# Prompt attention scores of a hybrid decoder layer: products of high and low fp32r parts, with the rope part stacked to 128 rows, in place of plain fp32 products

## The reference

```
def mla_scores(q_lat, q_rope, ckv, krope):
    s = einsum('bthc,bsc->bhts', q_lat, ckv) + einsum('bthr,bsr->bhts', q_rope, krope)
    return s * SM_SCALE
# prompt: 8 heads, 512 queries in 4 blocks of 128, causal mask, softmax, then p @ ckv
# q_lat and ckv have 128 channels, q_rope and krope have 64
```

## Time and profile before

| | |
|---|---|
| time, median of 3 runs | 1330.19 us (1328.15 to 1334.08) |
| profiled execution, span | 1334.3 us |
| PE busy | 1303.3 us, 98% |
| PE weight loads busy | 1234.6 us, 93% |
| DVE busy | 959.7 us, 72% |
| ACT busy | 602.2 us, 45% |
| POOL busy | 145.2 us, 11% |
| attention heads in the trace | 482.67 to about 722 us |

### The profile page before, as it was taken

One profiled execution on the slowest core, in us unless ns is written; L12 is line 12 of the kernel. 1 busy time (PEld: TensorE's weight loads), 2 busy tenths in 40 slices (PEclk: granted clock), 3 DMA queues, 4 the chain that ended last, 5 costly groups with the idle time before them and its releaser, 6 DMA issues.

```text
span 1334.3 us, 30517 instructions
## 1 busy us (share of the span) xinstructions
PE 1303.3 (98%) x11657; PEld 1234.6 (93%) x11657; DVE 959.7 (72%) x1847; ACT 602.2 (45%) x1144; POOL 145.2 (11%) x275
## 2 busy tenths in 40 slices
PE   9999999999999999899999999999999999999997
PEld 8999999999999978788888888889899999999996
DVE  5999899985487655555555665575889998988556
ACT  5455555653365344444345233234654555565323
POOL 0000000000003105455552000000000000000000
PEclk9999999999999999899999999999999999999999
DMA  4232223332256637777777313414253222333322
GB/s 165 94 121 102 96 95 123 110 97 90 65 194 219 218 94 207 228 211 237 214 228 250 140 64 129 153 48 168 75 193 96 96 96 96 100 107 116 101 87 101
DMA packets 86234, 180.85 MB, mean 136 GB/s; under 512 B 12681, under 2 KB 47498, under 8 KB 84042
## 3 DMA queue, kind: packets, MB, share of 16 engines
q1 hardware_dynamic: 77898, 162.12, 36.5%
q0 software_dynamic: 8192, 16.79, 4.4%
HBM read 162.29 MB, written 16.57 MB: 134 GB/s over the span
## 4 chain that ended last, share of the span: by engine, by line
PE 79%; DVE 9%; SPq 3%; DMA 3%; issue 3%; ACT 3%; DVEq 0%; ACTq 0%
PE acc L1096 20%; PE acc L1181 15%; PE acc L1018 11%; PE acc L855 6%; PE bank_a L1096 6%; PE acc L1042 4%; PE acc L927 2%; SPq L482 2%; DVE w_lo L2331 1%; PE bank_a L1251 1%; PE acc L1299 1%; PE bank_a L1281 1%; DMA w_raw<-in_w_gu 1%; SPq L475 1%; PE acc L1321 1%
## 5 line engine op out<-in xcount | busy, mean ns | idle before, releaser
L1096 PE MATMUL acc<-x_forms,pair_w 128*128 128x272 f32 x1728 | 273.1, 288 | 0.0
L1096 PEld LDWEIGHTS acc<-x_forms,pair_w 128*128 128x128 f32 x1728 | 244.3, 188 | 0.0
L1181 PE MATMUL acc<-x_hi,w_hi 128*128 128x272 f32 x656 | 198.9, 303 | 0.2 <-DVE gt L2806 0.2
L1181 PE MATMUL acc<-x_hi,w_lo 128*128 128x272 f32 x656 | 191.3, 292 | 0.0
L1181 PE MATMUL acc<-x_lo,w_hi 128*128 128x272 f32 x656 | 190.9, 291 | 0.0
L2331 DVE TENSOR_TENSOR w_lo<-w_raw,w_hi 128x1024 fp32r<-128x1024 f32 (+1 forms) x92 | 108.2, 1176 | 93.7 <-ACT w_hi L1627 93.2
L493 POOL DMA_DIRECT2D pg<-in_lat x256 | 137.9, 539 | 197.1 <-issue 132.8
L1627 ACT ACTIVATE w_hi<-w_raw 128x1024 fp32r<-128x1024 f32 (+1 forms) x92 | 93.0, 1018 | 92.0 <-PE acc L1181 38.9
L1181 PEld LDWEIGHTS acc<-x_hi,w_hi 128*128 128x128 f32 x656 | 124.1, 189 | 8.3 <-issue 6.4
L1181 PEld LDWEIGHTS acc<-x_lo,w_hi 128*128 128x128 f32 x656 | 124.2, 189 | 3.9 <-issue 3.0
L1181 PEld LDWEIGHTS acc<-x_hi,w_lo 128*128 128x128 f32 x656 | 123.9, 189 | 2.5 <-issue 2.2
(11 more groups left out here) (454 smaller groups left out, 2850.2 us busy)
## 6 DMA issues: line engine op xcount, KB each, us to landing
w_pair<-in_w_gu SPq DMA_DIRECT2D x68, 512.0 KB, 4.3
pg<-in_key_t SPq DMA_DIRECT2D x256, 96.0 KB, 2.5
w_raw<-in_w_in SPq DMA_DIRECT2D x44, 512.0 KB, 4.5
pg<-in_lat POOLq DMA_DIRECT2D x256, 64.0 KB, 2.8
w_raw<-in_w_dn SPq DMA_DIRECT2D x32, 448.0 KB, 3.3
w_raw<-in_w_gu SPq DMA_DIRECT2D x20, 512.0 KB, 3.5
block_raw<-in_w_dn SPq DMA_DIRECT2D x32, 256.0 KB, 3.6
g_mid<-gt SPq DMA_DIRECT2D x17, 272.0 KB, 2.9
```

The lines of the kernel that those rows point to most:

```text
L1096: ins = nc.tensor.matmul(bank, w[:, k * P:(k + 1) * P], v[:, k, :], start=start and k == 0 and term == 0, stop=k == KD // 2 - 1 and term == 2,
L1181: ins = nc.tensor.matmul(acc[0][:, a, 0:HT], w[:, i % 2, k * P:(k + 1) * P], v[:, k, a * HT:(a + 1) * HT], start=k == 0 and term == 0, sto ...
```

## The change

Each score is made by five fp32r products into one bank in place of two plain fp32 products: high query by high key, high by low, low by high, and two for the rope part. For these the rope query is stacked to 128 rows, its high part in one half of the partitions and its low part in the other, and the high rope key stands in both halves, as does the low one. So one product with the high key gives high by high and low by high, and one with the low key gives the rest.

ACT makes the high parts: `kvhi`, `krhi` once, `qlhi` in `latent_queries` (both copies after the second product), and `rope_high`. DVE makes the low parts: `split_keys` once, `latent_low`, which now frees the banks of `ql`, and `rope_low`. The low keys lie over the keys they are made from, so `split_keys` waits until the outputs `ckv` and `kr` are stored (`lat_out`) and the transposes are done. `rotate` works in place with two operations in place of four. For heads 1, 3 and 5 `next_query(h, 1)` moves ahead of both `dense(13)`, and `rotate` ahead of `take_output`. `wp_hi` moves to another place in SBUF to make room for the high keys.

```diff
@@ PE
             def two_scores(h, i):
                 if i == 0:
                     pe.wait_ge(a_read, A.taken(f"ql{h // 2}1"))
                     pe.wait_ge(qr_ready, h // 2 + 1)
-                    pe.wait_ge(kr_ready, 1)
-                bs = []
+                    pe.wait_ge(kv_split, 1)
+                hi, lo, rope = qlhi[:, h % 2, :], qllo[:, h % 2, :], q_rope[h % 2]
                 for c in (i, i + 1):
-                    n = (c + 1) * P
+                    q, n = slice(c * P, (c + 1) * P), (c + 1) * P
                     b = bank_a(f"sc{h}{c}")
-                    nc.tensor.matmul(b[:, 0:n], ql[:, h % 2, c * P:n], ckvT[:, 0:n], start=True, stop=False)
-                    bs.append((c, n, b))
-                for c, n, b in bs:
-                    g = slice(ROPE, P) if (h + c) % 2 else slice(0, ROPE)
-                    nc.tensor.matmul(b[:, 0:n], (qr_turned if c % 2 else qr)[g, c * P:n], krT[g, 0:n],
-                                     start=False, stop=True).then_inc(a_ready, 1)
+                    for term, (w, v) in enumerate(((hi, kvhi), (hi, kvlo), (lo, kvhi), (rope, krhi), (rope, krlo))):
+                        ins = nc.tensor.matmul(b[:, 0:n], w[:, q], v[:, 0:n], start=term == 0, stop=term == 4)
+                    ins.then_inc(a_ready, 1)
...
-                    dense(13)
-                    next_query(h, 1)
-                    dense(13)
+                    if h % 2:
+                        next_query(h, 1)
+                        dense(26)
+                    else:
+                        dense(13)
+                        next_query(h, 1)
+                        dense(13)
@@ ACT
-            nc.scalar.activation(krT[ROPE:P, 0:SEQ], krT[0:ROPE, 0:SEQ], ACT.Copy).then_inc(kr_ready, 1)
+            nc.scalar.activation(krhi[0:ROPE, :], krT[0:ROPE, 0:SEQ], ACT.Copy)
+            nc.scalar.activation(krhi[ROPE:P, :], krT[0:ROPE, 0:SEQ], ACT.Copy).then_inc(keys_hi, 1)
+            act.wait_ge(lat_ready, 1)
+            nc.scalar.activation(kvhi[:], ckvT[:, 0:SEQ], ACT.Copy).then_inc(keys_hi, 1)
...
             def latent_queries(p):
+                act.wait_ge(a_ready, A.filled(f"ql{p}1"))
                 for e in range(2):
-                    act.wait_ge(a_ready, A.filled(f"ql{p}{e}"))
-                    nc.scalar.activation(ql[:, e, :], A.bank(f"ql{p}{e}")[:], ACT.Copy).then_inc(a_read, 1)
+                    nc.scalar.activation(qlhi[:, e, :], A.bank(f"ql{p}{e}")[:], ACT.Copy).then_inc(ql_hi_done, 1)
...
+            def rope_high(p):
+                act.wait_ge(qr_rotated, p + 1)
+                nc.scalar.activation(q_rope[0][0:ROPE, :], qrx[0:ROPE, 0:SEQ], ACT.Copy)
+                nc.scalar.activation(q_rope[1][ROPE:P, :], qrx[ROPE:P, 0:SEQ], ACT.Copy).then_inc(qr_hi_done, 1)
...
             def sample_new(m):
                 sample_exp(m)
+                if m == 0:
+                    rope_high(0)
                 dense(12)
                 sample_turned(m)
...
+                    if h % 2:
+                        next_query(h, 1)
+                        dense(4)
+                        if h < HB - 1:
+                            rope_high(h // 2 + 1)
+                        dense(22)
@@ DVE
+            def split_keys():
+                dve.wait_ge(lat_out, 32)
+                dve.wait_ge(a_ready, A.filled("cts"))
+                dve.wait_ge(keys_hi, 2)
+                low = slice(0, ROPE)
+                nc.vector.tensor_tensor(krlo[ROPE:P, 0:SEQ], krT[low, 0:SEQ], f32(krhi[low, :]), ALU.subtract)
+                nc.vector.tensor_tensor(krlo[low, 0:SEQ], krT[low, 0:SEQ], f32(krhi[low, :]), ALU.subtract)
+                nc.vector.tensor_tensor(kvlo[:, 0:SEQ], ckvT[:, 0:SEQ], f32(kvhi[:]), ALU.subtract).then_inc(kv_split, 1)
+
+            split_keys()
             dense(48)
...
             def rotate(p):
-                link(nc.vector.tensor_tensor(qr[:, 0:SEQ], qrx[:, 0:SEQ], cos[:, 0:SEQ], ALU.mult))
+                q = qrx[:, 0:SEQ]
+                dve.wait_ge(vchain, own[0])
+                link(nc.vector.tensor_tensor(q, q, cos[:, 0:SEQ], ALU.mult))
+                nc.vector.tensor_tensor(q, q, tmp[:, 0:SEQ], ALU.subtract).then_inc(qr_rotated, 1)
+
+            def rope_low(p):
+                dve.wait_ge(qr_hi_done, p + 1)
                 low, high = slice(0, ROPE), slice(ROPE, P)
-                nc.vector.tensor_tensor(qr_turned[high, :], qr[low, 0:SEQ], tmp[low, 0:SEQ], ALU.subtract)
-                link(nc.vector.tensor_tensor(qr_turned[low, :], qr[high, 0:SEQ], tmp[high, 0:SEQ], ALU.subtract))
-                nc.vector.tensor_tensor(qr[:, 0:SEQ], qr[:, 0:SEQ], tmp[:, 0:SEQ], ALU.subtract).then_inc(qr_ready, 1)
+                nc.vector.tensor_tensor(q_rope[0][high, :], qrx[low, 0:SEQ], f32(q_rope[0][low, :]), ALU.subtract)
+                nc.vector.tensor_tensor(q_rope[1][low, :], qrx[high, 0:SEQ], f32(q_rope[1][high, :]), ALU.subtract)\
+                    .then_inc(qr_ready, 1)
+
+            def latent_low(p):
+                for e in range(2):
+                    dve.wait_ge(ql_hi_done, 2 * p + e + 1)
+                    nc.vector.tensor_tensor(qllo[:, e, :], A.bank(f"ql{p}{e}")[:], f32(qlhi[:, e, :]), ALU.subtract)\
+                        .then_inc(a_read, 1)
...
                 else:
-                    rotate(0)
+                    rope_low(0)
                 dense(18)
                 sample_sum(m)
 
             turn_rope(0)
+            rotate(0)
+            latent_low(0)
             dense(12)
...
-                    take_output(h)
                     if h % 2 and p + 1 < HB // 2:
                         rotate(p + 1)
+                    take_output(h)
...
-                    dense(26)
+                    if h % 2 and p + 1 < HB // 2:
+                        dense(4)
+                        latent_low(p + 1)
+                        rope_low(p + 1)
+                        dense(22)
+                    else:
+                        dense(26)
                     sample_sum(m1)
```

More of the change, by code:

```diff
@@ L203, in layer @@
         sq = put("sq", [P, 2, T])
-        wphi, cqhi = at("wp_hi", [P, 768], SG_AT, F32R), at("cq_hi", [P, 2, T], SQ_AT, F32R)
+        wp_hole = at("wp_hi", [P, 2, UNIT], W_HI_AT, F32R)
+        wphi = wp_hole[:, :, KD * P:UNIT]
+        cqhi = at("cq_hi", [P, 2, T], SQ_AT, F32R)
+        kvhi, krhi = (at(n, [P, SEQ], SG_AT + i * size([P, T]), F32R) for i, n in enumerate(("kv_hi", "kr_hi")))
         w_pair0 = at("w_pair0", [P, 2, 2 * QW], SQ_AT)
@@ L258, in layer @@
         wp = put("wp", [P, 1024])
-        qn = put("qn", [P, 2, SEQ])
-        ql = put("ql", [P, 2, SEQ])
+        qn_at = [cursor[0], cursor[0] + size([P, 2, SEQ])]
+        qn = [at(f"qn{i}", [P, SEQ], qn_at[1 - i]) for i in range(2)]
+        qlhi = put("ql_hi", [P, 2, SEQ], F32R)
+        qllo = put("ql_lo", [P, 2, SEQ], F32R)
+        kvlo = at("kv_lo", [P, T], cursor[0], F32R)
         ckvT = put("ckvT", [P, T])
+        krlo = at("kr_lo", [P, T], cursor[0], F32R)
         krT = put("krT", [P, T])
-        qr_turned = put("qr_turned", [P, SEQ])
+        q_rope = [at("q_rope0", [P, SEQ], RT_AT, F32R), put("q_rope1", [P, SEQ], F32R)]
         ckvtok = put("ckvtok", [P, NT + 1, P])
@@ L737, in _ @@
                 if p == 0:
-                    sp.wait_ge(kr_ready, 1)
+                    sp.wait_ge(kr_half, 2)
                     sp.wait_ge(lat_ready, 1)
-                    sp.dma_start(ckv_out, ckvT[:]).then_inc(small_out, 16)
-                    sp.dma_start(kr_out, krT[0:ROPE, :]).then_inc(small_out, 16)
+                    sp.dma_start(ckv_out, ckvT[:]).then_inc(lat_out, 16)
+                    sp.dma_start(kr_out, krT[0:ROPE, :]).then_inc(lat_out, 16)
                 dense(18)
@@ L829, in _ @@
             sp.wait_ge(x_out, 16 * 6)
-            sp.wait_ge(small_out, 16 * 5)
+            sp.wait_ge(small_out, 16 * 3)
+            sp.wait_ge(lat_out, 16 * 2)
         @block.tensor
@@ L1248, in query @@
                 for k in range(2):
-                    at_ = slice(k * 384 + m * P, k * 384 + (m + 1) * P)
-                    for term, (w, v) in enumerate(((wphi, cqhi), (wphi, cqlo), (wplo, cqhi))):
-                        ins = nc.tensor.matmul(b[:], w[:, at_], v[:, k, 0:SEQ],
+                    hi, lo = wphi[:, k, m * P:(m + 1) * P], wplo[:, k * 384 + m * P:k * 384 + (m + 1) * P]
+                    for term, (w, v) in enumerate(((hi, cqhi), (hi, cqlo), (lo, cqhi))):
+                        ins = nc.tensor.matmul(b[:], w, v[:, k, 0:SEQ],
                                                start=k == 0 and term == 0, stop=k == 1 and term == 2)
@@ L2060, in split_pair @@
                     act.wait_ge(a_ready, A.filled(f"q{p - 1}2"))
-                nc.scalar.activation(wphi[:], wp[:, 0:768], ACT.Copy).then_inc(wp_hi, 1)
+                nc.scalar.activation(wphi, wp[:, 0:768].rearrange("p (k n) -> p k n", k=2), ACT.Copy).then_inc(wp_hi, 1)
             split_pair(0)
@@ L2959, in turn_rope @@
```

(8 more changed lines are left out.)

14 lines of the change are left out of this document (8 added, 6 removed).

## The result

The changed kernel takes 1336.2 us (median of 20 runs, 1331.36 to 1343.12), the kernel before 1331.4 us (20 runs, 1328.15 to 1335.8): a ratio of 1.0032, 95% interval 1.0022 to 1.0041. That is a small loss, within the 0.5% that the prediction took as the bound of "no change". The 1336.2 us lie 5.4 us above the predicted 1330.8 and just beyond the upper end of the range, 1336. The profiled execution took 1338.89 us, its span 1337.2 us. Three executions far outside the rest (2637 and 4446 us of the kernel before, 2106 us in run 3) are left out of all medians.

The account below looks back on a forecast made before the run. Two page queues beside a nearly full TensorE bound the stage: the late start (+3.3 us), less 0.95 a head where the queues let it show, gives +0.6, span 1334.9, and with 4.1 less 1330.8 us, range 1324 to 1336.

Parts of the forecast that it names:

- the three waits: TensorE waits 3 us ahead of head 0, over 4.0 us for the pair weights, 3 us for a last-values page.
- the missing wait of GpSimd: Near 625, GpSimd's wait of 1.48 us for TensorE disappears and GpSimd is 1.2 us late.
- signs of being wrong: Faster page issue than 0.83 and 0.94 us, no wait ahead of head 0, or clock 0.50 at several stage places.
- Rival (a): Attention stage: TensorE alone decides, page queues are faster unprofiled or margins larger; -4.3 us, 1325.9; chance 0.25.
- rival (c): Scores: fp32r products of 128 columns cost as much as plain fp32; +1.9 us, 1332.1; chance 0.08.
- Scores: Each head's score products on TensorE fall from 4.24 to 3.28 us, about 0.95 saved, 7.6 over eight heads.
- Start of head 0: Side operations on DVE and ACT delay TensorE's sample values by 3.3 us; bounds 0 and +5.8.
- rival (b): Clock falls in the new wait before head 0, +3.1 us, or also at the last values, +5.6, 1335.8; chance 0.12.
- The wait for wp: In head 2, TensorE's wait for the pair weights grows from 4.0 to 5.9 us.
- The key split: Once before the heads, extra ACT copies and DVE subtractions cost nothing; without cover 2.1 us.
- the later pairs: At heads 2, 4 and 6, extra DVE and ACT operations cost nothing, margin 1.3 us; above, 1 us each.
- From the span to the runs: Runs' median stays 4.1 us under the profiled span, as before: span 1334.9 gives 1330.8 us.

Follow-up runs that it names:

- run 3: Changed kernel with the scores as plain fp32 products on the high parts alone, all side operations kept: 1335.8 us, ratio 1.003 to the kernel before.
- run 2: Changed kernel with only the high-by-high product of each score's five, so the scores are wrong: 1336.55 us, ratio 1.0033 to the kernel before.
- run 4: Changed kernel with four neighbouring cache pages to one transfer, without the page table: 1326.6 us, ratio 0.9949 to the kernel before.
- run 5: Kernel before with four neighbouring cache pages to one transfer, without the page table: 1329.12 us, ratio 0.997 to the unedited kernel before.
- run 10: Changed kernel with side operations behind the sample softmax, wp from ACT's queue, one table-addressed transfer per page split over SP and GpSimd: 1324.08 us, ratio 0.9926.
- run 11: Kernel before with wp loaded from ACT's queue and one table-addressed transfer per page, split over SP and GpSimd: 1330.83 us, ratio 0.9981.
- run 1: Changed kernel with DVE's sample maximum and ACT's turned probabilities ahead of the side operations at head 0: 1332.47 us, ratio 0.9996 to the kernel before.
- run 9: Changed kernel with the side operations behind the sample softmax, wp from ACT's queue and four neighbouring pages to one transfer: 1321.85 us, ratio 0.9919.
- run 7: Changed kernel with the side operations behind the sample softmax and wp reloaded from ACT's queue: 1331.22 us, ratio 0.9995 to the kernel before.

## Why the prediction was off by 5 us

**Its mechanism held.** TensorE's saving was eaten by the two page queues, and the three waits and the missing wait of GpSimd stand where it put them. Runs 2 and 3 show that the products are not in the time, runs 4, 5, 10 and 11 that they are once the queues have slack, and run 1 that the order at the start made the loss. Of the 5.4 us by which the forecast was low, 2.3 are the span and 3.1 the step from the span to the runs; both follow below. One of its own signs of being wrong did show: a clock at 0.50 at two places in the stage, 483.2 to 493.4 and 558.2 to 565.1. Rival (a), TensorE alone, is refuted by runs 2 and 3, and rival (c) by the trace: a 128-column product took 0.115 us, not the price of plain fp32.

**Scores.** 0.95 us a head was forecast, 1.1 measured (28.14 against 29.25 in the earlier trace rows). The scores themselves give 4.24 - 3.49 = 0.75: they took 3.49 us, not 3.28, above all as some first products hold longer (0.28 us instead of 0.175 at 384 columns). The other 0.35 lie around them; which products gave them is not shown.

**Start of head 0: the term that was mis-sized.** The sample values come at 484.93, against 481.23 before: 3.7 us, of which 0.45 stood already ahead of the queries (470.68 against 470.23 in the earlier trace rows). The 3.25 left are the forecast 3.3. But the prediction put the fall of the clock in this wait into rival (b), with a chance of 0.12, and this half of (b) is what happened: it gave +3.1 us on the span, and 2.9 were measured. Head 0's scores start 4.85 us late, the wp load 4.90, GpSimd's batch at 566.96 4.57, its last page 4.52, where the prediction had +3.3, +2.35, +2.35 and +1.2. The second half of (b), a fall at the last values, did not come in this execution; it came in that of run 1, which starts earlier. Run 1 took the wait away and with it 3.7 us; with the queues out of the way (runs 4 and 9) it is 4.0 us of the stage. The Trainium skill (TensorE: Matmul & The Clock Gate, section "HAM oscillation — how this bites in real kernels") says that each burst behind an idle gap starts cold. The trace agrees here for a gap of 2.84 us, shorter than the one of 3.86 that the prediction had to go by; behind the gap of 2.32 us in run 7 the clock stayed at 1.00.

**The wait for wp** was 4.46 us, not 5.9, since TensorE reached it late too. The key split and the later pairs cost nothing that shows: no wait for their operations stands in the stage.

**From the span to the runs: the larger miss.** The span rose by 2.9 us (0.6 forecast), the median by 4.8. The prediction carried over the 4.1 us by which the runs of before lay under their profiled span; the changed kernel's median lies only 1.0 us under its own. The profiled execution of before took longer than any of those runs: its span of 1334.3 us is a time of about 1336.0 (the changed kernel's time is 1.7 above its span), and the 20 runs end at 1335.8. Without queue waits the span falls by 6.9 us (1334.3 to 1327.4), the median by 2.3. The prediction gave no reason why the runs of both kernels should lie equally far under their spans.

**What stays open.** Over the changed kernel's 20 runs the mean granted clock goes from 0.997 (1331.36 us) to 0.988 (1343.12), so much of the spread goes with the clock. Which wait let it fall in which run is not known, as only one execution has a trace. How much of the median loss is clock was not tried by itself. All of it need not be: run 3, with the same start, lost as much at a mean granted clock of 0.996, that of the kernel before.

## What to carry to other kernels

A busy TensorE does not prove that TensorE sets the end: follow the queue that issues the loads from its first to its last transfer, and if it hardly pauses in a whole stage, make its transfers fewer before making the products cheaper. Operations that come with cheaper products belong behind the small chain that TensorE waits for next; an order of two engines' lists cost 3.7 us here, while what eight heads saved did not show at all until the queues had slack. Two repairs that draw on the slack of the same queue do not add.

## What the runs showed of the hardware that was not expected

- Products of fp32r start 0.115 us apart at 128 and at 256 columns, 0.175 at 384 and 0.232 at 512 (changed kernel, head 1): here 128 columns cost as much as 256.
- The same kind of wait lowered the clock for different lengths: 2.84 us of idle time was followed by 10.2 us at 0.50 in the changed kernel and by 6.8 us in run 3 (the clock is 0.77 in the window from 482 and 0.81 in the one from 489), while behind the wait of 2.32 us in run 7 it stayed at 1.00. In run 1 two waits of 1.82 and 1.02 us close together were followed by 10.2 us at 0.50.
- From one page to the next GpSimd's issues lie 0.90 us apart for 64 KB in the changed kernel (the median of the stage; 0.96 is the mean from 566.96 on) and 0.91 us for the page of 160 KB in run 10, so that a transfer of two and a half times the size is issued in the same time.
